# Gate and up of ten feed-forwards in rows, with 512 moving columns, and the hidden rows turned group by group

## What is computed

```python
def swiglu(h, w_in, w_out):
    gate, up = jnp.split(h @ w_in, 2, axis=-1)
    return (jax.nn.silu(gate) * up) @ w_out

for i in range(DEPTH):                      # DEPTH = 4, D_MODEL = 1024, D_FF = 2816
    g = norm_g[i]
    x = x + 0.5 * rms_norm(swiglu(rms_norm(x, g[0]), ff1_w_in[i], ff1_w_out[i]), g[1])
    ...
    x = x + 0.5 * rms_norm(swiglu(rms_norm(x, g[4]), ff2_w_in[i], ff2_w_out[i]), g[5])
...
gate, up = jnp.split(rmsnorm(x, norm_ffn[layer]) @ w_gate_up[layer], 2, axis=-1)
x = x + (jax.nn.silu(gate) * up) @ w_down[layer]
```

## Time and profile before

| | us |
|---|---|
| median of 3 runs | 3237.32 |
| lowest and highest run | 3235.91, 3238.64 |
| the profiled execution, its own time | 3236.72 |
| its span, first to last instruction | 3234.9 |
| PE busy (matmuls) | 3128.8 |
| DVE busy | 1873.1 |
| ACT busy | 1474.7 |

### The profile page before, as it was taken

The page is one execution under the profiler, slowest core; times in us unless marked ns, Lnnn a source line. Parts: engine busy times, 40 slices in busy tenths (PEclk is TensorE's granted clock), DMA queues, the critical chain, the costliest instruction groups (busy, mean ns, idle before and its releaser), DMA issues.

```text
span 3234.9 us, 53035 instructions
## 1 busy us (share of the span) xinstructions
PE 3128.8 (97%) x22719; PEld 2968.7 (92%) x22719; DVE 1873.1 (58%) x2541; ACT 1474.7 (46%) x2285; POOL 78.9 (2%) x153
## 2 busy tenths in 40 slices
PE   8999999999999998899999999999999999989999
PEld 8989998989999988898999999998888989988897
DVE  5556555546555556754555555576755556776554
ACT  4445444434544444444444554434445443454443
POOL 0000000000000000000000000100000000000000
PEclk9999999999999999999999999999899999999999
DMA  6563555555555554255556355654144567414453
GB/s 215 183 209 112 175 183 183 181 177 183 181 189 178 183 181 151 86 182 193 179 182 215 105 176 186 192 183 144 47 157 139 184 191 200 155 40 143 139 184 134
DMA packets 434398, 533.92 MB, mean 165 GB/s; under 512 B 27330, under 2 KB 398452, under 8 KB 434164
## 3 DMA queue, kind: packets, MB, share of 16 engines
q1 hardware_dynamic: 421220, 512.22, 49.0%
q10 hardware_dynamic: 12944, 18.31, 1.7%
HBM read 528.33 MB, written 1.11 MB: 164 GB/s over the span
## 4 chain that ended last, share of the span: by engine, by line
PE 91%; DVE 4%; ACT 2%; DMA 1%; issue 1%; SPq 0%; POOL 0%; POOLq 0%; DVEq 0%; ACTq 0%
PE bank L683 90%; PE bank L943 1%; ACT sb_parts L1178 1%; DMA sb_ring<-in_w_xq_dram 1%; DVE sb_parts L1609 0%; DVE sb_sc L1763 0%; PE bank L721 0%; DMA sb_ring<-in_w_out_dram 0%; DMA sb_ring<-in_w_branch_nsa_dram 0%; DMA sb_ring<-in_ff_w_in_dram 0%; ACT sb_sc L1276 0%; ACT sb_prT L1189 0%; DVE sb_nmax L1765 0%; ACT sb_oT_high L1152 0%; DVE sb_oT_low L1697 0%
## 5 line engine op out<-in xcount | busy, mean ns | idle before, releaser
L1609 DVE TENSOR_TENSOR sb_parts<-sb_ring,sb_parts 128x2048 fp32r<-128x2048 f32 x480 | 1098.6, 2293 | 603.0 <-ACT sb_parts L1178 601.5
L683 PE MATMUL bank<-sb_hT_high,sb_parts 128*128 128x256 f32 x7808 | 1411.1, 283 | 0.1
L683 PEld LDWEIGHTS bank<-sb_hT_high,sb_parts 128*128 128x128 f32 x7808 | 1220.0, 192 | 0.4 <-issue 0.4
L1178 ACT ACTIVATE sb_parts<-sb_ring 128x2048 fp32r<-128x2048 f32 x480 | 912.6, 1908 | 537.7 <-PE bank L683 426.6
L683 PE MATMUL bank<-sb_hT_low,sb_parts 128*128 128x256 f32 x3904 | 1104.8, 283 | 0.0
L683 PEld LDWEIGHTS bank<-sb_hT_low,sb_parts 128*128 128x128 f32 x3904 | 749.5, 192 | 0.0
L683 PE MATMUL bank<-sb_parts,sb_hidden_high 128*128 128x512 f32 x1760 | 543.9, 390 | 0.0
L683 PE MATMUL bank<-sb_parts,sb_hT_high 128*128 128x256 f32 (+3 forms) x2560 | 484.5, 291 | 12.1 <-DVE sb_hT_low L1711 9.9
L683 PEld LDWEIGHTS bank<-sb_parts,sb_hT_high 128*128 128x128 f32 x2560 | 410.6, 197 | 20.2 <-DVE sb_hT_low L1711 17.4
L683 PEld LDWEIGHTS bank<-sb_parts,sb_hidden_high 128*128 128x128 f32 x1760 | 329.6, 188 | 75.0 <-issue 0.6
L1241 ACT ACTIVATE sb_prT<-bank 128x256 f32<-128x256 f32 x220 | 84.6, 385 | 635.6 <-PE bank L683 635.5
(11 more groups left out here) (212 smaller groups left out, 2144.5 us busy)
## 6 DMA issues: line engine op xcount, KB each, us to landing
sb_ring<-in_ff_w_in_dram SPq DMA_DIRECT2D x176, 1024.0 KB, 5.1
sb_ring<-in_ff_w_out_dram SPq DMA_DIRECT2D x88, 1024.0 KB, 5.0
sb_ring<-in_w_gate_up_dram SPq DMA_DIRECT2D x44, 1024.0 KB, 5.1
sb_ring<-in_w_in_dram SPq DMA_DIRECT2D x42, 1024.0 KB, 5.3
sb_ring<-in_a_w_qkv_dram SPq DMA_DIRECT2D x24, 1024.0 KB, 5.2
sb_ring<-in_w_down_dram SPq DMA_DIRECT2D x22, 1024.0 KB, 5.0
sb_ring<-in_c_w_qkv_dram SPq DMA_DIRECT2D x12, 1024.0 KB, 5.1
sb_ring<-in_a_w_o_dram SPq DMA_DIRECT2D x8, 1024.0 KB, 5.2
```

The lines of the kernel that those rows point to most:

```text
L683: return nc.tensor.matmul(o, lhsT, rhs, start=start, stop=stop)
L1178: nc.scalar.activation(halves(n, slice(0, filled(n))).high, ring[:, raw_in[n], 0:filled(n)], ACT.Copy) \
L1609: V.tensor_tensor(both.low, ring[:, raw_in[n], 0:filled(n)], both.high.bitcast(F32), ALU.subtract) \
```

## The change

Part 2 of a feed-forward is made in rows too. The features 256 to 2815 form five groups of 512. For each group gate and up come one after the other; a chunk is now half of the k-tiles (4 of 8) by 512 features, still 1 MB. `hT` is stationary, 512 weight columns move, and a whole bank holds gate or up of one token tile. SiLU and multiplication work on 128x512 instead of 128x256, and `silu` and `hid_f` use the whole of `prT` and `sc`. All 22 hidden tiles are now in rows and are turned on PE by `turned_hidden`: those of group g-1 after the first chunk of group g, into banks 4 to 7, and the last group after the first chunk of the output product, into banks 0 to 3. ACT and DVE make `hidT.high` and `hidT.low` from those banks, two tiles at a time. `first_rows` and the order of the output product stay. In the diff, "..." in the three `ffn` and in `hidden_high` and `hidden_low` stands for the removed lines too, which are printed above.

```diff
+GROUPS_F = 1 + (D_FF - 256) // 512
...
+    def halves(key, m, c0, n):
+        for h in range(2):
+            rows((key[0], key[1], key[2], h), m[h * 4 * P:(h + 1) * 4 * P, c0:c0 + n], 4, whole=True)
     def ffn(key, w_in, w_out):
-        for j in range(KF // 2):
-            cols((key, "gate", j), w_in, j * 256, 256)
-            cols((key, "up", j), w_in, D_FF + j * 256, 256)
+        cols((key, "gate", 0), w_in, 0, 256)
+        cols((key, "up", 0), w_in, D_FF, 256)
+        for g in range(1, GROUPS_F):
+            for kind, c0 in (("gate", 0), ("up", D_FF)):
+                halves((key, kind, g), w_in, c0 + 256 + (g - 1) * 512, 512)
         rows((key, "out"), w_out, 2)
...
-        silu = prT[:, :, 0:S]
-        hid_f = sc[:, :, 0:S]
+        silu = prT
+        hid_f = sc
...
-                        pe.wait_ge(dve_step.sem, dve_step.at((key[0], "h", 2 * n + 1)))
+                        pe.wait_ge(dve_read.sem, dve_read.at((key[0], "hid", (n + 1) // 2, (n + 1) % 2 if n else 0)))
                     arrived(ckeys[n])
...
+                    if second and n == 1:
+                        second()
...
...
...
+                first_rows(st, [(st, "gate", 0, 0), (st, "up", 0, 0)], lambda t: (st, "up", 0, t))
+                for g in range(1, GROUPS_F):
+                    for kind in ("gate", "up"):
+                        banks = [G.take(pe, (st, kind, g, t)) for t in range(NT)]
+                        for h in range(2):
+                            ckey = (st, kind, g, h)
+                            arrived(ckey)
+                            s = view(ckey)
                             for t in range(NT):
...
+                                for k in range(4):
+                                    ins = split_mm(banks[t][:, :], hT[:, 4 * h + k, t * P:(t + 1) * P], s[:, k, :],
+                                                   h == 0 and k == 0, h == 1 and k == 3)
+                                if h == 1:
+                                    ins.then_inc(matmul_done.sem, matmul_done.next((st, kind, g, t)))
+                            if h == 0:
+                                ins.then_inc(matmul_done.sem, matmul_done.next((st, kind, g, "half")))
+                            chunk_end[ckey] = (st, kind, g, 1 if h else "half")
+                            if kind == "gate" and h == 0:
+                                turned_hidden(st, g - 1, YB)
+                wide_gemm(st[0], [(st, "out", m) for m in range(KF // 2)], (st, "y"), hidT, set_up if st == stages[0] else None,
+                          lambda: turned_hidden(st, GROUPS_F - 1, G))
+            def turned_hidden(st, g, banks):
+                for t in range(NT):
+                    pe.wait_ge(dve_read.sem, dve_read.at((st, "up", g, t)))
+                for b in range(2 if g else 1):
+                    bank = banks.take(pe, (st, "hid", g, b))
+                    for c in range(2):
+                        for t in range(NT):
+                            ins = nc.tensor.transpose(bank[:, c * S + t * P:c * S + (t + 1) * P],
+                                                      hid_f[:, t, (2 * b + c) * P:(2 * b + c + 1) * P], ident[:, :])
+                    ins.then_inc(transposed.sem, transposed.next((st, "hid", g, b)))
...
...
+                for t in range(NT):
+                    ahead((st, ("gate", "up")[t], 0, 0))
+                    act.wait_ge(matmul_done.sem, matmul_done.at((st, "up", 0, t)))
+                    nc.scalar.activation(silu[:, t, 0:S], G.of((st, "up", 0, t))[:, 0:S], ACT.Silu) \
+                        .then_inc(act_read.sem, act_read.next((st, "up", 0, t)))
+                for g in range(1, GROUPS_F):
+                    ahead((st, "gate", g, 0))
+                    hidden_high(st, g - 1)
+                    ahead((st, "gate", g, 1))
+                    for t in range(NT):
+                        act.wait_ge(matmul_done.sem, matmul_done.at((st, "gate", g, t)))
+                        act.wait_ge(dve_read.sem, dve_read.at((st, "up", g - 1, t)))
+                        nc.scalar.activation(silu[:, t, :], G.of((st, "gate", g, t))[:, :], ACT.Silu) \
+                            .then_inc(act_read.sem, act_read.next((st, "gate", g, t)))
+                    for h in range(2):
+                        ahead((st, "up", g, h))
                 for m in range(KF // 2 - 1):
                     ahead((st, "out", m))
+                    if m == 0:
+                        hidden_high(st, GROUPS_F - 1)
                     if m == 4 and st == stages[0]:
                         set_up()
                 turn(st)
...
+            def hidden_high(st, g):
+                for b in range(2 if g else 1):
+                    act.wait_ge(transposed.sem, transposed.at((st, "hid", g, b)))
+                    k = 2 * (2 * g - 1 + b) if g else 0
+                    copy(hidT.high[:, k:k + 2, :], G.of((st, "hid", g, b))[:, :].rearrange("p (c s) -> p c s", c=2)) \
+                        .then_inc(act_step.sem, act_step.next((st, "hid", g, b)))
...
...
+                for t in range(NT):
+                    ahead((st, ("gate", "up")[t], 0, 0))
+                    dve.wait_ge(act_read.sem, act_read.at((st, "up", 0, t)))
+                    V.tensor_tensor(hid_f[:, t, 0:S], silu[:, t, 0:S], G.of((st, "up", 0, t))[:, S:2 * S], ALU.mult) \
+                        .then_inc(dve_read.sem, dve_read.next((st, "up", 0, t)))
+                for g in range(1, GROUPS_F):
+                    ahead((st, "gate", g, 0))
+                    hidden_low(st, g - 1)
+                    ahead((st, "gate", g, 1))
+                    for h in range(2):
+                        ahead((st, "up", g, h))
+                    for t in range(NT):
+                        dve.wait_ge(act_read.sem, act_read.at((st, "gate", g, t)))
+                        dve.wait_ge(matmul_done.sem, matmul_done.at((st, "up", g, t)))
+                        V.tensor_tensor(hid_f[:, t, :], silu[:, t, :], G.of((st, "up", g, t))[:, :], ALU.mult) \
+                            .then_inc(dve_read.sem, dve_read.next((st, "up", g, t)))
+                    if st == stages[0] and g in (1, 2):
+                        (set_up_lines if g == 1 else set_up_angles)()
                 for m in range(KF // 2 - 1):
                     ahead((st, "out", m))
+                    if m == 0:
+                        hidden_low(st, GROUPS_F - 1)
                     if m == 4 and st == stages[0]:
                         set_up_rest()
                 turn(st)
...
+            def hidden_low(st, g):
+                for b in range(2 if g else 1):
+                    dve.wait_ge(act_step.sem, act_step.at((st, "hid", g, b)))
+                    k = 2 * (2 * g - 1 + b) if g else 0
+                    V.tensor_tensor(hidT.low[:, k:k + 2, :], G.of((st, "hid", g, b))[:, :].rearrange("p (c s) -> p c s", c=2),
+                                    hidT.high[:, k:k + 2, :].bitcast(F32), ALU.subtract) \
+                        .then_inc(dve_read.sem, dve_read.next((st, "hid", g, b)))
```

More of the change, by code:

```diff
@@ L853, in branch_gemm, with wide_gemm @@
                         ins.then_inc(matmul_done.sem, matmul_done.next((key, t, h)))
-            def wide_gemm(st, ckeys, key, src, between=None):
+            def wide_gemm(st, ckeys, key, src, between=None, second=None):
                 final = key[1] == "y"
@@ L897, in ffn @@
             def ffn(st):
[L898 to L914, removed]
-                            for t in range(NT):
-                                ins = nc.tensor.transpose(bank[:, c * S + t * P:c * S + (t + 1) * P],
-                                                          hid_f[:, t, c * P:(c + 1) * P], ident[:, :])
-                        ins.then_inc(transposed.sem, transposed.next((st, "hid")))
@@ L919, in ffn @@
-                wide_gemm(st[0], [(st, "out", m) for m in range(KF // 2)], (st, "y"), hidT, set_up if st == stages[0] else None)
+                first_rows(st, [(st, "gate", 0, 0), (st, "up", 0, 0)], lambda t: (st, "up", 0, t))
[6 more added lines that the diff above has]
+                            s = view(ckey)
+                            for t in range(NT):
+                                for k in range(4):
[8 more added lines that the diff above has]
+                                turned_hidden(st, g - 1, YB)
@@ L1254, in ffn @@
                 turn(st)
-            def hidden_high(st, i):
-                act.wait_ge(dve_read.sem, dve_read.at((st, "h", i)))
-                copy(hidT.high[:, i, :], hid_f[:, i % 3, :]).then_inc(act_step.sem, act_step.next((st, "hh", i)))
+            def hidden_high(st, g):
[4 more added lines that the diff above has]
+                        .then_inc(act_step.sem, act_step.next((st, "hid", g, b)))
             def attention(st):
@@ L1718, in ffn @@
                 norm_low(st, 1)
-                for i in range(KF):
-                    ahead((st, "gate" if i % 2 == 0 else "up", i // 2, 0))
-                    if i == 3:
```

(18 more changed lines are left out.)

22 lines of the change are left out of this document (2 added, 20 removed).

## The result

The changed kernel took **3212.27 us** (median of four runs, 3210.16 to 3214.53) against 3237.49 of the kernel before in runs beside it: ratio 0.9923, 95% interval 0.9905 to 0.9940. That is 25.2 us less, where I had forecast 9.5 less and a range that ended at 3220. The sign was right, the size was not.

A forecast was written before the change was run, and what follows sets the result against it. PE's instruction count times spacing was taken to bound each feed-forward. 3236.7 - 53.5 (wider matmuls) + 44.0 (transposes) = 3227.2, plus 0.6 for the median: 3227.8 us, range 3220 to 3238.

The forecast's parts named there:

- What bounds the kernel: Inside a feed-forward, time is the number of PE instructions times their start-to-start spacing; other engines matter only if late.
- the first term: Gate and up: 480 matmuls of 512 columns replace 960 of 256 per feed-forward, saving 53.5 us over ten.
- The bound of 54: Upper limit on the saving from wider gate and up matmuls, taking 0.2287 us for each: 54 us.
- The transposes: Forty more transposes of hidden tiles on PE per feed-forward, 0.110 us each: 44.0 us more over ten.
- the rival: Edges of 60 transpose blocks: each shows one more weight load, about 0.11 us, giving 3234.4 us; 14%.
- the rival of cheaper blocks: In each of 60 transpose blocks one load that now shows is hidden, 6.6 us less: 3221.2 us; 4%.
- The new wait: PE waits after a group's first chunk for the previous group's multiplications; at least 0.80 us to spare, priced at nothing.
- ACT and DVE: Per 22.9 us group, DVE works 11.9 us and ACT 10.0; half idle, so their changed work costs nothing.
- A pair costs what a wide one costs: Rival: in gate and up 512 columns take twice 0.120 us, nothing pays for the transposes, +44.0, 3281 us; 5%.
- the two terms: On PE in ten feed-forwards: wider gate and up matmuls save 53.5 us, added transposes cost 44.0 us.
- the runs scatter by 1.4: Assumed run-to-run scatter of 1.4 us, used when setting the chances of faster, same and slower.

## Why the prediction was wrong in size

- **What bounds the kernel:** right. PE's instructions times their spacing set a feed-forward, before and after.
- **The step that failed** is the first term, where it says "the spacing of 512-column ones is in the same stage, in the output product": 60.19 / 263 = 0.2289. I took a price from instructions of the same shape, type and stage, and checked that bank rotation did not matter. I did not check where their stationary tile lies. The new matmuls have `hT` as stationary tile, at a multiple of 128 bytes, and take 0.2267. The term is 4800 x (0.2400 - 0.2267) = **64 us, not 53.5**. The bound of 54 that I gave it was no bound, since it came from the same matmuls. The right row was in the trace of before, in the branch stages, where 512-column matmuls with `hT` stationary already ran:

```profile
2250.38 0.61 PE L683 MATMUL bank<-sb_parts,sb_hT_high 128*128 128x512 f32 x2
...
2260.58 0.61 PE L683 MATMUL bank<-sb_parts,sb_hT_high 128*128 128x512 f32 x2
```

   10.20 / 45 = 0.2267. By that row the sum would have been 3237.3 - 64 + 44 = 3217, below my range and 5 from the result.
- **The transposes:** right. 0.110 each in the forecast, 0.109 measured; with the edges 4.54 for a stage instead of 4.40, so 45.4 us instead of 44.0. The cost beyond proportion is 0.03 to 0.08 for a block, less than the 0.11 that the rival gave it, and nothing was hidden, as the rival of cheaper blocks would have it.
- **The new wait:** right. In the stage at 350 us the second multiplication of group 0 starts at 359.68 and lasts 0.41, the transposes start at 360.86: 0.77 us to spare, where I had 0.80. PE waited for none of the 440 transposes.
- **ACT and DVE:** right; the wide multiplications take 0.683, the copies 0.597 and the wide SiLUs 0.599, as priced.
- **A pair costs what a wide one costs:** it does not: 0.2267 against 2 x 0.1200. Of the rule I had cited beside it (the Trainium skill, "TensorE: Matmul & The Clock Gate", section "Wait — 56ns, not 53.3ns?", about 2.5 ns over N ÷ 2.4 GHz) the runs show the form and not the size: the surplus is the same for each matmul at the two widths, 0.1200 - 0.1067 = 13.3 ns at 256 columns and 0.2267 - 0.2133 = 13.3 at 512 (stationary tile at a multiple of 128 bytes), five times the figure of the page. Why it is that large here stays open; no run varied it.
- **The rest:** 64.0 - 45.4 = 18.6, and the feed-forwards lost 18.5. The medians of the three comparisons differ by 22.4 to 25.2. These further 4 to 7 us lie outside the changed stages, in the profiles mostly in the branch stages; I had no term for them, and their cause stays open. That the sign came out right is no luck: it rests on the two terms, and both were found in the trace. With that scatter (the kernel before alone spread over 7.7 us in 15 runs), my "the runs scatter by 1.4", read from three runs, was too small as well.

## What to carry to other kernels

A matmul's price should come from rows in which its stationary tile is the same one, or one that lies alike, and not only from rows of the same shape; where two such groups differ by even 1%, multiply that by the count before choosing. In this kernel, bound by the spacing of its matmuls, each had the same surplus over its columns, so joining two of 256 columns pays 13 ns, eight such pairs pay for one transpose of 0.109 us, and here 12 pairs were saved for each. Before counting on more, look at where the stationary tiles begin: here it was worth 6 us from 64 bytes to none, and one run each at 32 and 96 bytes gave back 18 of the rewrite's 25.

## What was not expected of the hardware

- The place of the stationary tile sets the spacing of 512-column matmuls: 0.2268 us at a multiple of 128 bytes, 0.2290 at 64 past it, 0.2334 at 32 or 96 past it, with float32r operands and 128 x 128 tiles.
- The surplus of a matmul over its columns at 2.4 GHz is 13.3 ns at both widths, 256 and 512, with the stationary tile at a multiple of 128 bytes.
- Transposes back to back cost 0.109 us each beside wide matmuls, and the change from matmuls to transposes and back 0.03 to 0.08 us on top.
- The same 1100 matmuls of a branch stage took 133.0 or 136.0 us in two executions of one program; the granted clock of one stretch of 20 us in them was 0.91 or 0.75.
